# Queries and keys of the dilated attention: both parts of x as one moving operand, evacuated in two halves

## The reference, cut to what matters

```
h = rmsnorm_2(x, norm_mix_g[i])
z = h @ w_in[i]
qa, ka, va, qb, kb, vb, ga, gb = jnp.split(z, split_at, axis=-1)
qb = qb.reshape(b, s, N_HEADS_B, HEAD_DIM_B)      # 12 heads of 64: 768 columns
kb = kb.reshape(b, s, N_HEADS_B, HEAD_DIM_B)      # 768 columns
y_a = mixer_a(qa, ka, va, ...) @ w_out_a[i]       # full attention, with rotary embedding
y_b = mixer_b(qb, kb, vb, rel_bias) @ w_out_b[i]  # dilations 1, 4 and 16
```

## Time and profile before

| | us |
|---|---|
| median of 3 runs (lowest, highest) | 970.94 (970.88, 971.11) |
| profiled execution, own time | 972.82 |
| its span | 971.1 |
| TensorE busy | 962.8 (99%) |
| VectorE busy | 658.6 (68%) |
| ScalarE busy | 493.0 (51%) |

### The profile page before, as it was taken

How to read it: one execution, slowest core, us unless ns; L and a number is a source line. 1 busy time by engine, 2 the same in 40 slices (tenths; PEclk the granted TensorE clock), 3 DMA queues, 4 the chain that set the end, 5 groups by cost and what they waited for, 6 DMA issues and landing times.

```text
span 971.1 us, 13084 instructions
## 1 busy us (share of the span) xinstructions
PE 962.8 (99%) x5366; PEld 828.5 (85%) x5366; DVE 658.6 (68%) x932; ACT 493.0 (51%) x595; POOL 60.9 (6%) x129
## 2 busy tenths in 40 slices
PE   9999999999999999999999999999999999999997
PEld 8888888888889878888888889988888888888886
DVE  5877776655578967665666658867766766566665
ACT  5465554444447855444444445465554544444454
POOL 3441000000001001000000012000000000000000
PEclk9999999999999999999999999999999999999999
DMA  8563667677462325767665556453266465555551
GB/s 250 199 211 133 196 178 233 214 199 240 173 215 92 128 87 189 226 190 205 210 204 208 183 163 217 145 193 118 81 230 212 153 217 173 197 193 181 190 193 54
DMA packets 115251, 176.57 MB, mean 182 GB/s; under 512 B 5548, under 2 KB 78200, under 8 KB 115192
## 3 DMA queue, kind: packets, MB, share of 16 engines
q1 hardware_dynamic: 115016, 175.54, 55.6%
q10 hardware_dynamic: 176, 0.20, 0.1%
HBM read 174.03 MB, written 1.70 MB: 181 GB/s over the span
## 4 chain that ended last, share of the span: by engine, by line
PE 99%; DMA 1%; DVE 0%; SPq 0%; ACT 0%; issue 0%; DVEq 0%; ACTq 0%
PE ps L368 95%; PE ps L372 3%; DMA x<-in_x 1%; DVE M L1235 0%; SPq L2954 0%; ACT M L2152 0%; DVE M L2129 0%; DVE x L1235 0%; DVEq L2101 0%; ACTq L2754 0%; DVE st L2129 0%
## 5 line engine op out<-in xcount | busy, mean ns | idle before, releaser
L368 PE MATMUL ps<-whi,RR 128*128 128x512 f32 (+1 forms) x1556 | 397.5, 387 | 0.0
L1235 DVE TENSOR_TENSOR wlo<-raw,whi 128x1024 fp32r<-128x1024 f32 (+1 forms) x323 | 373.3, 1198 | 27.2 <-ACT whi L2152 26.9
L2152 ACT ACTIVATE whi<-raw 128x2048 fp32r<-128x2048 f32 (+1 forms) x161 | 301.2, 1873 | 164.4 <-PE ps L368 139.6
L368 PEld LDWEIGHTS ps<-whi,RR 128*128 128x128 f32 x1556 | 283.8, 188 | 55.5 <-issue 0.9
L368 PE MATMUL ps<-RR,whi 128*128 128x512 f32 (+1 forms) x1264 | 261.9, 351 | 0.0
L368 PEld LDWEIGHTS ps<-RR,whi 128*128 128x128 f32 x1264 | 201.6, 191 | 26.7 <-issue 1.5
L368 PE MATMUL ps<-wlo,RR 128*128 128x512 f32 (+1 forms) x778 | 220.5, 385 | 0.0
L368 PEld LDWEIGHTS ps<-wlo,RR 128*128 128x128 f32 x778 | 144.2, 188 | 29.4 <-DVE wlo L1235 0.2
L1235 DVE TENSOR_TENSOR M<-M,ps 128x512 f32<-128x512 f32 (+1 forms) x57 | 38.7, 683 | 172.9 <-ACT M L2152 168.6
L368 PEld LDWEIGHTS ps<-RR,wlo 128*128 128x128 f32 x1016 | 138.3, 191 | 9.1 <-DVE wlo L1235 0.7
L368 PE MATMUL ps<-RR,wlo 128*128 128x256 f32 x1016 | 144.7, 283 | 0.0
(11 more groups left out here) (109 smaller groups left out, 422.9 us busy)
## 6 DMA issues: line engine op xcount, KB each, us to landing
raw<-in_w_up SPq DMA_DIRECT2D x32, 1024.0 KB, 6.1
raw<-in_w_down SPq DMA_DIRECT2D x32, 1024.0 KB, 5.3
raw<-in_w_ff SPq DMA_DIRECT2D x32, 1024.0 KB, 5.2
raw<-in_w_in SPq DMA_DIRECT2D x23, 1024.0 KB, 5.0
raw<-in_a_w_in SPq DMA_DIRECT2D x10, 1024.0 KB, 5.2
raw<-in_a_w_out SPq DMA_DIRECT2D x4, 1024.0 KB, 5.3
raw<-in_b_w_q SPq DMA_DIRECT2D x4, 1024.0 KB, 5.4
raw<-in_b_w_out SPq DMA_DIRECT2D x4, 1024.0 KB, 4.9
```

The costliest lines, as they stand in the source:

```text
L368: return pe.matmul(out, lhsT, rhs, start=start, stop=stop, skip_group_check=True)
L1235: return dve.tensor_tensor(out, a, b, op)
L2152: return act.activation(out, in_, ACT.Copy, **k)
```

## The change

The six blocks are made by `gemm_up` in place of `gemm_a`. Each then takes two PSUM banks. ScalarE gets two evacuation steps, `ev_qb` and `ev_kb`, that copy the first 256 columns of both banks to their turned places in `M`. VectorE's step waits for that copy, adds the other 256 columns of both banks in one instruction of 512 elements, marks the banks read, waits for its own addition, and scales in place: the keys in one instruction of 512 elements, the queries in two of 256. `di_scores` now waits for the scaled results.

```
+    def di_q(self, f):
+        out = self.M[:, 2 * f:2 * f + 512].rearrange("p (i t) -> p i t", i=2)
+        return out.rearrange("p i (two t) -> p i two t", two=2), "p i (t two) -> p i two t"
+
+    def di_k(self, f):
+
+        out = self.M[:, 1536 + 2 * f:2048 + 2 * f].rearrange("p (i t) -> p i t", i=2)
+        if f == 0:
+            return out.rearrange("p i (t two) -> p i t two", two=2), "p i (t two) -> p i t two"
+        return out.rearrange("p i (two t) -> p i two t", two=2), "p i (t two) -> p i two t"
...
-        for w in due(K.empty(("qb", 512)), K.empty(("kb", 512))):
+        for w in due(K.at("qb", 512), K.at("kb", 512)):
...
-    run_all((gemm_a(("qb",), W2, 1536, 768, hT, ready), 1))
-    run_all((gemm_a(("kb",), W2, 2304, 768, hT, ready), 1))
+    run_all((gemm_up(("qb",), W2, 1536, 768, ready), 1))
+    run_all((gemm_up(("kb",), W2, 2304, 768, ready), 1))
...
     def ev_k(f):
         tile = ("kb", f)
-        for w in due(K.full(tile), K.at("x_lnf"), *rb(4)):
-            dve.wait_ge(*w)
-        for a in range(0, 512, 256):
-            out, b, r = M[:, 1536 + 2 * f + a:1792 + 2 * f + a], K.bank(tile)[:, a:a + 256], RB[:, a:a + 256]
-            if f:
-                t = tt(halves_of(out), by_parity(b), by_parity(r), ALU.mult)
-            else:
-                t = tt(out, b, r, ALU.mult)
+        out, turn = V.di_k(f)
+        for w in due(K.at("kb_high", f), *rb(4)):
+            dve.wait_ge(*w)
+        t = tt(out, out, K.pair(tile, 512)[:, :, T:2 * T].rearrange(turn, two=2), ALU.add)
         t.then_inc(*K.emptied(tile))
+        for w in due(K.empty(tile)):
+            dve.wait_ge(*w)
+        r = RB[:, :].rearrange("p (i t) -> p i t", i=2).rearrange(turn, two=2)
+        tt(out, out, r, ALU.mult).then_inc(*K.up("kb", f))
 
     def ev_q(f):
         tile = ("qb", f)
-        for w in due(K.full(tile), K.at("x_lnf"), *rb(4)):
-            dve.wait_ge(*w)
-        for a in range(0, 512, 256):
-            t = stt(halves_of(M[:, 2 * f + a:2 * f + a + 256]), by_parity(K.bank(tile)[:, a:a + 256]), 0.125,
-                    by_parity(RB[:, a:a + 256]), ALU.mult, ALU.mult)
+        out, turn = V.di_q(f)
+        for w in due(K.at("qb_high", f), *rb(4)):
+            dve.wait_ge(*w)
+        t = tt(out, out, K.pair(tile, 512)[:, :, T:2 * T].rearrange(turn, two=2), ALU.add)
         t.then_inc(*K.emptied(tile))
+        for w in due(K.empty(tile)):
+            dve.wait_ge(*w)
+        for i in range(2):
+            t = stt(out[:, i], out[:, i], 0.125, by_parity(RB[:, 0:T]), ALU.mult, ALU.mult)
+        t.then_inc(*K.up("qb", f))
...
+    def ev_qb(f):
+        tile = ("qb", f)
+        out, turn = V.di_q(f)
+        for w in due(K.full(tile), K.at("x_lnf")):
+            act.wait_ge(*w)
+        copy(out, K.pair(tile, 512)[:, :, 0:T].rearrange(turn, two=2)).then_inc(*K.up("qb_high", f))
+
+    def ev_kb(f):
+        tile = ("kb", f)
+        out, turn = V.di_k(f)
+        for w in due(K.full(tile), K.at("x_lnf")):
+            act.wait_ge(*w)
+        copy(out, K.pair(tile, 512)[:, :, 0:T].rearrange(turn, two=2)).then_inc(*K.up("kb_high", f))
+
     def products_b():
-        yield from gemm_a(768, lambda f: None)
-        yield from gemm_a(768, lambda f: None)
+        yield from gemm_a(768, ev_qb)
+        yield from gemm_a(768, ev_kb)
```

## The result

The changed kernel takes 973.84 us (median of 15 runs, 973.23 to 975.12) against 971.32 for the kernel before (15 runs, 970.55 to 972.74). The ratio of the means is 1.0024, with a 95% interval of 1.0017 to 1.0031: slower, by 2.5 us between the medians. The forecast was 973.3 and slower.

What follows compares the result with a forecast made beforehand. TensorE bounds, VectorE has no reserve: 0.45 + 3.48 = 3.93 us delay, plus 0.1 wait, puts B6's low matmuls at 620.3, not 617.90; 970.94 + 2.4 = 973.3 us, TensorE's saving spent waiting. Range 971.2 to 974.8.

Steps and rivals of the forecast that it cites:

- The bound and where to look: Between B3 and B6: TensorE, 99% busy, is the bound; VectorE is busy 17.18 of 17.28 us, without reserve.
- three pauses: TensorE waits for VectorE's low parts at B3, B5 and B6: about 1.0, 1.5 and 1.0 us.
- TensorE's saving: Twelve halves of 16 matmuls in place of 24: 0.0925 us less each, 1.11 us in all.
- VectorE's evacuations: Each grows by 0.72 us for queries, 0.66 for keys: 3.48 us ahead of the low part of B6.
- The start: First evacuation, of B0: VectorE waits for ScalarE's copy, queued behind its square, and starts 0.45 us later.
- The wait for a semaphore: TensorE's wait for VectorE's low part of B6: 0.1 us added, between nothing and 0.2.
- What is late next: After B6's low part: last key evacuation hidden with 0.25 us to spare; B8's raw weights and bank pairs also in time.
- Full saving: Rival: VectorE's delay stays under 1.63 us, never reaches TensorE, and 1.11 us are saved, 969.8 us; 11 in 100.
- late raw weights: Rival: B8's DMA takes 10.7 us, delaying ScalarE's copy for `rotated(4)`; 1.2 us more, 974.5; 7 in 100.
- The granted clock: Rival, with late scaled keys: pauses of 1 to 1.5 us lower the clock, another 5.6 us, 979; 4 in 100.

Runs made afterwards that it cites:

- scaling left out: Changed kernel without VectorE's second evacuation step, the scaling, so output is wrong: 970.01 us against 970.82 for the kernel before, ratio 0.9990.
- more VectorE work: Kernel before, plus two more 256-element multiplications into unused columns after each of six evacuations: 972.75 us against 970.82, ratio 1.0017.
- with the copies: Kernel before, plus ScalarE's six copies into unused columns, which VectorE awaits before its old evacuations: 970.79 us against 971.20, ratio 0.9999.
- keys only: Kernel before with the change for the keys alone (B3 to B5), queries made and evacuated as before: 971.32 us against 970.82, ratio 1.0005.
- keys only with two low parts early: Kernel before with the keys changed, and VectorE making B2's low part before evacuating B0, B5's before B3: 970.92 us against 971.20, ratio 0.9992.
- GpSimd kernel: Changed kernel with the row-scale multiplication for B0 to B4 moved from VectorE to GpSimd: 975.81 us against 970.82 for the kernel before, ratio 1.0049.
- queries only: Kernel before with the change for the queries alone (B0 to B2), keys made and evacuated as before: 973.10 us against 971.20, ratio 1.0020.
- low part of B2 early: Changed kernel with VectorE making B2's low part before it evacuates B0: 972.82 us against 971.20 for the kernel before, ratio 1.0013.

## Why the prediction was right

- **The bound and where to look.** Right. TensorE set the time, and VectorE, though at 68% over the span, was the engine without reserve in this stretch. The three pauses stand at B3, B5 and B6, as forecast. From start to start of the rows they are 1.28, 1.38 and 0.88 us (at B3, 599.47 - 596.35 less the 1.84 of the high matmuls), 3.54 together; 1.0, 1.5 and 1.0 were forecast, 3.5 together. The idle times in brackets, 1.11, 1.21 and 0.72, leave out what the profile counts as the end of the high matmuls.
- **TensorE's saving.** 1.11 us forecast, 1.05 measured where nothing hides it (scaling left out), 10.9 ns for each of 96 matmuls. By the Trainium skill's 2.5 ns (TensorE: Matmul & The Clock Gate, "Wait — 56ns, not 53.3ns?") it would be 0.24 us, an estimate; the trace does not agree for these matmuls. In the changed kernel the saving was spent waiting, as forecast.
- **VectorE's evacuations.** Right to the hundredth. From the first evacuation to the end of the low part of B6 it is 616.27 - 587.38 = 28.89 us before and 618.71 - 586.34 = 32.37 after: 3.48 us more, and 3.48 was forecast. The wait between the addition and the scaling costs what the MLP's pair showed: 0.71 us from the one to the other, against 0.61 from the scaling to the next (606.50 to 607.11). With the scaling left out, the same addition has no wait behind it, and the next instruction starts after 0.60 (603.25 to 603.85 in that kernel): the wait costs 0.11 us. The Trainium skill (VectorE: DVE Perf Modes, "The DRAIN you can't avoid") says that the semaphore costs nothing extra, with which these rows do not agree, and also that a next op which is not held starts earlier, with which they do.
- **The start.** Mis-sized: 0.45 us forecast, 0.77 measured (6.72 us after B0 in place of 5.95). The mechanism was right, VectorE waits for a copy that waits for ScalarE's square. But the square started 584.58 - 579.62 = 4.96 us after B0 and not 586.01 - 581.43 = 4.58, since ScalarE's row there begins when the raw weights of B1 land (579.80), and that was 0.38 us later relative to B0. I had carried over its position from the trace before. Nothing here ties that shift to the change. In the five kernels that make B0 as before (before, more VectorE work, with the copies, keys only, keys only with two low parts early) the row begins between 0.26 us before B0 and 0.45 us behind it; in the changed one it is 0.18 behind. So the size of this term is in part chance of the profiled execution. The 0.32 us is most of what the trace's delay, 2.67 us at the low part of B6 and 2.76 at `di_scores(0)`, has above the 2.4 forecast. The rest is that the first low matmuls behind a pause take 0.1 us more (1.22 in place of 1.12).
- **The wait for a semaphore.** 0.1 taken, 0.05 to 0.06 seen.
- **What is late next.** The last keys were scaled in time (619.34 + 0.69 = 620.03, before 620.34), the raw weights and the bank pairs too: no pause of TensorE has any other releaser.
- **The rivals.** Full saving did not happen. The condition that the prediction gave for it, a delay under 1.63 us, was wrong: such a delay only keeps the kernel from being slower. To save, TensorE must come 1.05 us earlier and still find the low part, so 0.58 us are left, and with the scaling left out the delay of 0.52 just fitted. The case of late raw weights did not arise; ScalarE waited 1.05 us for those of B8 (high part at 617.81), and had it done before it was needed. The granted clock stayed at 1.00 over pauses of 1.1 and 1.2 us, so that rival did not arise here. It fell only behind the pause of 2.15 us in the GpSimd kernel, and there it cost about 1.6 us and not 5.6 (from 619.25 to the second half of B6 at 624.38 in the GpSimd kernel, 5.13 us, against 622.30 - 618.76 = 3.54 in the changed one).

What stays open is why a matmul costs some 11 ns beyond its columns here. No run varied its size alone.

## What to carry to other kernels

When a change takes work from the engine that bounds the kernel and gives some to another, look at the other engine's busy share in that very stretch, and write down for each thing it delivers by when it is needed: here 68% over the span was 99% in the stretch, and 1.63 us to spare decided over 3.5 us of new work. A delay costs only what goes beyond the smallest reserve, so half a change can be almost free where the whole is not. What the bounding engine saves is taken off that reserve too. Before giving the work up, look for idle time just ahead of the row: the same instructions in another order were worth 1.5 us.

## What was not expected of the hardware

**GpSimd and VectorE.** A multiplication of GpSimd over 512 columns of SBUF lengthened VectorE's instructions with two SBUF inputs beside it by 1.03 to 1.12 us, four times, and took 1.34, 2.23, 2.12 and 2.50 us itself. The first one, beside a reduction with one input, took 1.31 us and left that at 1.48. Taken one by one, the VectorE records around the second row of GpSimd above are these:

```profile
600.79 1.22 DVE L1246 TENSOR_TENSOR wlo<-raw,whi 128x1024 fp32r<-128x1024 f32 x1
...
601.92 2.34 DVE L1246 TENSOR_TENSOR wlo<-raw,whi 128x1024 fp32r<-128x1024 f32 x1
```

The two engines take turns. The VectorE instruction that was running when GpSimd began keeps its 1.22 us and ends at 602.01; GpSimd ends 1.17 us behind that, at 603.18; VectorE's next one takes 2.34 and ends 1.08 us behind GpSimd. At the other three places GpSimd ends 1.15 to 1.17 us behind the VectorE instruction it met, too, so its row is long when that one was long. What the two share was not tried apart.

**The start of the kernel.** The runs of the kernel before lie in two groups, near 971 and near 972.5 us, on the same chip. The profiled one belongs to the upper group. The timelines of TensorE at the start, of the kernel before and of the changed kernel:

```profile
6.73 1.12 PE L372 MATMUL ps<-ident,x 128*128 128x128 f32 x4 [1.07 <-DMA x<-in_x]
7.50 2.06 PE L368 MATMUL ps<-RR,whi 128*128 128x256 f32 x8
```

```profile
6.43 0.66 PE L383 MATMUL ps<-ident,x 128*128 128x128 f32 x4 [0.78 <-DMA x<-in_x]
6.85 1.19 PE L379 MATMUL ps<-RR,whi 128*128 128x256 f32 x8
```

The same eight matmuls take 2.06 us in one and 1.19 in the other, behind a wait of 1.07 and 0.78 us for x, and the 1.8 us by which B0 starts apart (581.43, 579.62) arise there: by the 25th microsecond the same row begins at 24.79 and at 22.94. Two other profiled executions show the row of 2.06, queries only (974.41 us) and the changed kernel with the low part of B2 early (973.76), both above the median of their kernel; the rest show 1.19 or 1.20. Among these, the kernel before with more VectorE work (973.51, above its median too) waits another 0.93 us for GpSimd there. The windows view gives a granted clock of 1.00 over 4 to 12 us of the kernel before, so the clock's record does not show it. This is why the two profiled spans differ by 1.0 us only, where the medians differ by 2.5. The medians are mixed too: of the 15 runs each in the result, 7 of the kernel before and 3 of the changed one belong to the upper group.
